# A decoder block on one core: the last half tile of gates handed over between blocks, and a merge with deeper, earlier loads

## The reference, cut to what matters

```python
h = rms_norm(x, g_mix) * (1.0 + sc1) + sh1
(a_q, a_k, a_v, conv_in, c_q, c_k, c_v, c_r, c_low,
 d_q, d_k, d_v, gate_logits) = split(h @ w_in)
y_a = dilated_attention_mixer(a_q, a_k, a_v, q_gain, k_gain) @ w_br_a
y_b = conformer_conv_mixer(conv_in, ...) @ w_br_b
y_c = gla_mixer(c_q, c_k, c_v, c_r, c_low, ...) @ w_br_c
y_d = stick_breaking_mixer(d_q, d_k, d_v) @ w_br_d
gates = sigmoid(gate_logits).reshape(bsz, seq, 4, 1024)
merged = gates[:,:,0]*y_a + gates[:,:,1]*y_b + gates[:,:,2]*y_c + gates[:,:,3]*y_d
x = x + gt1 * (merged @ w_out)
h = rms_norm(x, g_mlp) * (1.0 + sc2) + sh2
x = x + gt2 * (square(relu(h @ w_up)) @ w_down)
```

## Time and profile before

| what | us |
|---|---|
| median of the three runs | 2075.84 (2072.96 to 2077.95) |
| the profiled execution, its own time | 2075.17 |
| its span (first to last instruction) | 2073.4 |
| TensorE busy | 1989.8 (96% of the span) |
| front block, until TensorE starts in the stick block | 0 to 511.42 |
| stick block | to 711.35 |
| GLA block | to 914.53 |
| window block | to 1145.29 |
| close block: dense, y and merge | to 1309.1 |
| close block: output projection and MLP | to 2073.4 |

### The profile page before, as it was taken

The page is one execution under the profiler, slowest core; times in us unless marked ns, Lnnn a source line. Parts: engine busy times, 40 slices in busy tenths (PEclk is TensorE's granted clock), DMA queues, the critical chain, the costliest instruction groups (busy, mean ns, idle before and its releaser), DMA issues. The chain is left out here.

```text
span 2073.4 us, 24243 instructions
## 1 busy us (share of the span) xinstructions
PE 1989.8 (96%) x9416; PEld 1589.7 (77%) x9416; DVE 1239.4 (60%) x1631; ACT 695.8 (34%) x1087; POOL 249.6 (12%) x148
## 2 busy tenths in 40 slices
PE   5999999999999999989999788999999999999999
PEld 4787888877766677865788677788788888888887
DVE  6547575110465477343456377577877777777776
ACT  5311111132576432255553333333222212222221
POOL 0112122112221153125000000000000000000000
PEclk9999999999999999999999999999999999999999
DMA  8354554324211331252132655500211211111112
GB/s 277 86 172 128 169 155 119 92 82 149 86 45 51 130 106 47 87 217 103 45 116 67 205 187 177 177 11 10 92 46 46 67 46 51 52 61 41 51 41 92
DMA packets 197339, 206.47 MB, mean 100 GB/s; under 512 B 9402, under 2 KB 154938, under 8 KB 197226
## 3 DMA queue, kind: packets, MB, share of 16 engines
q1 hardware_dynamic: 197056, 204.85, 31.2%
q10 hardware_dynamic: 170, 0.07, 0.0%
HBM read 157.57 MB, written 47.32 MB: 99 GB/s over the span
## 5 line engine op out<-in xcount | busy, mean ns | idle before, releaser
L661 PE MATMUL dn_ps<-h_hi,dn_hi 128*128 128x512 f32 (+1 forms) x1120 | 460.4, 411 | 24.2 <-PEq L60 11.5
L663 PE MATMUL dn_ps<-h_hi,dn_lo 128*128 128x512 f32 (+1 forms) x1120 | 440.9, 394 | 0.0
L662 PE MATMUL dn_ps<-h_lo,dn_hi 128*128 128x512 f32 (+1 forms) x1120 | 440.8, 394 | 0.0
L661 PEld LDWEIGHTS dn_ps<-h_hi,dn_hi 128*128 128x128 f32 (+1 forms) x1120 | 211.4, 189 | 95.3 <-issue 44.9
L663 PEld LDWEIGHTS dn_ps<-h_hi,dn_lo 128*128 128x128 f32 (+1 forms) x1120 | 211.1, 188 | 48.3
L662 PEld LDWEIGHTS dn_ps<-h_lo,dn_hi 128*128 128x128 f32 (+1 forms) x1120 | 211.6, 189 | 45.8 <-issue 4.3
L139 POOL TENSOR_TENSOR dn_lo<-dn_raw,dn_hi 128x1024 fp32r<-128x1024 f32 (+1 forms) x69 | 169.3, 2455 | 620.8 <-ACT dn_hi L135 610.2
L156 ACT ACTIVATE dn_out<-dn_ps 128x512 f32<-128x512 f32 (+1 forms) x138 | 81.7, 592 | 450.3 <-PE dn_ps L663 442.6
L1505 DVE TENSOR_TENSOR tl_x<-tl_x,mg_ps_y 128x512 f32<-128x512 f32 x256 | 175.8, 687 | 89.4 <-PE mg_ps_y L663 82.6
L661 PE MATMUL mg_ps_y<-tl_slot_hi,tl_u_hi 128*128 128x512 f32 x480 | 187.0, 390 | 1.2 <-issue 1.2
L663 PE MATMUL mg_ps_y<-tl_slot_hi,tl_u_lo 128*128 128x512 f32 x480 | 186.8, 389 | 0.0
(11 more groups left out here) (375 smaller groups left out, 3406.1 us busy)
## 6 DMA issues: line engine op xcount, KB each, us to landing
dn_raw<-w_in_dram SPq DMA_DIRECT2D x70, 512.0 KB, 4.4
ada<-w_ada_dram SPq DMA_DIRECT2D x24, 1024.0 KB, 7.8
proj<-dn_out SPq DMA_DIRECT2D x72, 256.0 KB, 2.3
logits<-dn_out SPq DMA_DIRECT2D x64, 256.0 KB, 2.2
mg_gate<-logits SPq DMA_DIRECT2D x32, 512.0 KB, 4.9
tl_unit<-w_up_dram SPq DMA_DIRECT2D x64, 256.0 KB, 2.9
tl_unit<-w_down_dram SPq DMA_DIRECT2D x64, 256.0 KB, 2.7
wa_qk<-proj SPq DMA_DIRECT2D x6, 1024.0 KB, 15.9
```

Source lines behind the costliest of these rows:

```text
L661: nc.tensor.matmul(out, w_hi[:, t, :], x_hi[:, t, :], start=begin, stop=False, skip_group_check=reopened)
L662: nc.tensor.matmul(out, w_hi[:, t, :], x_lo[:, t, :], start=False, stop=False, skip_group_check=reopened)
L663: mm = nc.tensor.matmul(out, w_lo[:, t, :], x_hi[:, t, :], start=False, stop=end, skip_group_check=reopened)
```

## The change: what it does

At the end of each of the first four blocks the last half tile of dense work is computed, but its copy, the split that hangs on it and its store are moved to the head of the next block. GLA takes 23 half tiles instead of 22 and close 3 instead of 4; stick and window keep 20 and 18, so window's are now numbers 43 to 60. In GLA `lower` still runs up to the block's full count, so it includes the low part that half tile 42 calls for. In the merge, the logits get a ring of five buffers (three of `gate` and two more), half tiles are stored between the y loads, logits 0 and branch weights 1 are loaded among the y, logits 1 to 3 follow the last three y, later logits are issued four ahead, and `low_branch(n+1)` moves behind `merge(4n+1)`. Several buffers have new addresses so that branch weights 1 no longer lie on h. One wait of a later slot split (on `gain_done`) goes. The mathematics is the same.

```diff
@@ stage_front, SyncE and ScalarE
-                    for h in range(NH):
-                        dense.store(sp, j - 2, h)
+                    dense.store(sp, j - 2, 0)
+                    if j - 2 < N_TILES - 1:
+                        dense.store(sp, j - 2, 1)
...
-                for h in range(NH):
-                    dense.copy(act, j, h)
-                dense.split(act, j + 2)
+                dense.copy(act, j, 0)
+                if j < N_TILES - 1:
+                    dense.copy(act, j, 1)
+                    dense.split(act, j + 2)
@@ stage_stick, stage_gla, stage_window, stage_close
-    FROM = dense.served
+    FROM = dense.piece // 3
@@ stage_stick
-            dense.move(sp, FROM + HALVES)
+            dense.store(sp, dense.first_gate - 1, 1)
+            dense.move(sp, FROM + HALVES - 1)
...
+            dense.copy(act, dense.first_gate - 1, 1)
+            dense.split(act, dense.first_gate + 1)
...
-                dense.serve(act, FROM + halves_before(n))
-            dense.serve(act, FROM + HALVES)
+                dense.serve(act, FROM + min(HALVES - 1, halves_before(n)))
+            dense.serve(act, FROM + HALVES - 1)
@@ stage_gla
-    PREPARE, LEVEL, STATE, NORM = 8, 8, 2, 4
+    PREPARE, LEVEL, STATE, NORM = 8, 8, 2, 5
...
-            dense.move(sp, FROM + PREPARE + LEVEL + STATE + NORM)
+            dense.move(sp, FROM + PREPARE + LEVEL + STATE + NORM - 1)
...
-            dense.serve(act, FROM + PREPARE + LEVEL + STATE + NORM)
+            dense.serve(act, FROM + PREPARE + LEVEL + STATE + NORM - 1)
@@ stage_window
-            dense.move(sp, FROM + PREPARE + DURING + MERGING)
+            dense.move(sp, FROM + PREPARE + DURING + MERGING - 1)
...
-            dense.serve(act, FROM + PREPARE + DURING + MERGING)
+            dense.serve(act, FROM + PREPARE + DURING + MERGING - 1)
@@ stage_close
-    GATE_RING = 3
+    GATE_RING, LOGIT_RING = 3, 5
...
             def load_branch(n):
-                if n == 1:
-                    sp.wait_ge(dense.done, NH * len(dense.tiles))
...
             def load_logits(m):
-                if m < GATE_RING:
-                    sp.wait_ge(y_lo_ready, Y_TILES)
-                else:
-                    sp.wait_ge(used, m - GATE_RING + 1)
-                sp.dma_start(gate[:, m % GATE_RING], k.logits[m * P:(m + 1) * P, :]).then_inc(g_in[m % GATE_RING], 16)
+                if 1 <= m <= GATE_RING:
+                    sp.wait_ge(y_lo_ready, Y_TILES - GATE_RING + m)
+                elif m == LOGIT_RING - 1:
+                    sp.wait_ge(dense.done, NH * len(dense.tiles))
+                elif m >= LOGIT_RING:
+                    sp.wait_ge(used, m - LOGIT_RING + 1)
+                for h in range(NH):
+                    sp.wait_ge(dense.stored[h], 16 * (dense.first_gate + m - dense.early + 1))
+                sp.dma_start(logits_at(m), k.logits[m * P:(m + 1) * P, :]).then_inc(g_in[m % LOGIT_RING], 16)
...
             for t in range(Y_TILES):
                 load_y(t)
+                if t == 2:
+                    dense.move(sp, FROM)
+                    load_logits(0)
+                if t in (3, 6):
+                    dense.move(sp, FROM + min(HALVES, t // 3))
+                if t == 4:
+                    load_branch(1)
+            for m in range(1, GATE_RING + 1):
+                load_logits(m)
             dense.move(sp, FROM + HALVES)
-            load_branch(1)
-            for h in range(NH):
-                sp.wait_ge(dense.stored[h], 16 * (len(dense.tiles) - dense.early))
+            load_logits(LOGIT_RING - 1)
             for m in range(M):
-                load_logits(m)
+                if m >= 1 and m + LOGIT_RING - 1 < M:
+                    load_logits(m + LOGIT_RING - 1)
...
-                if m % 4 == 2 and m // 4 + 1 < N_TILES:
+                if m % 4 == 1 and m // 4 + 1 < N_TILES:
                     low_branch(m // 4 + 1)
```

More of the change, by code:

```diff
@@ L690, in stage_close @@
         merged = at("mg_merged", 0, [P, KT, S])
-        b_raw = [at("mg_br_raw0", 172, [P, Y_TILES, P]), at("mg_br_raw1", 32, [P, Y_TILES, P])]
-        b_hi = [at("mg_br_hi0", 177, [P, Y_TILES, P], F32R), at("mg_br_hi1", 37, [P, Y_TILES, P], F32R)]
-        b_lo = [at("mg_br_lo0", 182, [P, Y_TILES, P], F32R), at("mg_br_lo1", 42, [P, Y_TILES, P], F32R)]
+        b_raw = [at("mg_br_raw0", 172, [P, Y_TILES, P]), at("mg_br_raw1", 204, [P, Y_TILES, P])]
+        b_hi = [at("mg_br_hi0", 177, [P, Y_TILES, P], F32R), at("mg_br_hi1", 209, [P, Y_TILES, P], F32R)]
+        b_lo = [at("mg_br_lo0", 182, [P, Y_TILES, P], F32R), at("mg_br_lo1", 214, [P, Y_TILES, P], F32R)]
         y_hi = at("mg_y_hi", 92, [P, Y_TILES, S], F32R)
@@ L696, in stage_close @@
         gate = at("mg_gate", 187, [P, GATE_RING, S])
-        diag = [at("tl_diag1", 48, [P, KT, P]), at("tl_diag2", 204, [P, KT, P])]
+        gate_more = [at("mg_gate_first", 199, [P, S]), at("mg_gate_last", 44, [P, S])]
+        diag = [at("tl_diag1", 48, [P, KT, P]), at("tl_diag2", 32, [P, KT, P])]
         mj_hi = at("tl_mj_hi", 48, [P, 2, KT, P], F32R)
@@ L701, in stage_close @@
         raw = at("tl_raw", 64, [P, 2, KT * P])
-        raw_rest = [at("tl_raw_row4", 172, [P, D]), at("tl_raw_row5", 176, [P, D]), at("tl_raw_row6", 180, [P, D]), at("tl_raw_row7", 199, [P, D])]
+        raw_rest = [at("tl_raw_row4", 172, [P, D]), at("tl_raw_row5", 176, [P, D]), at("tl_raw_row6", 180, [P, D]), at("tl_raw_row7", 36, [P, D])]
         row_hi = [at("tl_wo_hi", 72, [P, 2, D], F32R), at("tl_wo_hi_rest", 92, [P, KT - 2, D], F32R)]
@@ L710, in stage_close @@
         xn_second = at("tl_xn_second", 36, [P, D])
-        SLOT_KB = (40, 44, 204, 212, 16, 20)
+        SLOT_KB = (44, 204, 208, 212, 16, 20)
         slot_hi = [at(f"tl_slot_hi{i}", kb, [P, 4, P], F32R) for i, kb in enumerate(SLOT_KB)]
@@ L722, in stage_close @@
         u_lo = [at("tl_u_lo", 56, [P, BF, S], F32R), at("tl_u_lo_last", 80, [P, BF, S], F32R)]
-        gain2 = at("tl_gain2", 208, [P, D])
+        gain2 = at("tl_gain2", 40, [P, D])
         ps_y = ctx.enter_context(nc.psum_tensor("mg_ps_y", [P, Y_RING, NH, HALF], F32))
@@ L727, in stage_close @@
         b_in = sems(nc, ctx, "mg_b_in0", "mg_b_in1")
-        g_in = sems(nc, ctx, *(f"mg_in{t}" for t in range(GATE_RING)))
+        g_in = sems(nc, ctx, *(f"mg_in{t}" for t in range(LOGIT_RING)))
         (y_hi_ready, y_lo_ready, b_hi_ready, b_lo_ready, y_done, gate_ready, gated, used) = sems(
@@ L754, in stage_close, with logits_at @@
         QUADS = [(0, 0), (1, 0), (0, 1), (1, 1)]
+        def logits_at(m):
+            s = m % LOGIT_RING
+            return gate[:, s % GATE_RING] if 1 <= s <= GATE_RING else gate_more[s // (LOGIT_RING - 1)][:, :]
         def pair(p):
@@ L976, in squash @@
             def squash(m):
-                act.wait_ge(g_in[m % GATE_RING], 16 * (m // GATE_RING + 1))
-                nc.scalar.activation(gate[:, m % GATE_RING], gate[:, m % GATE_RING], ACT.Sigmoid).then_inc(gate_ready, 1)
+                act.wait_ge(g_in[m % LOGIT_RING], 16 * (m // LOGIT_RING + 1))
+                nc.scalar.activation(logits_at(m), logits_at(m), ACT.Sigmoid).then_inc(gate_ready, 1)
             def split(t):
@@ L1304, in merge @@
                 y = ps_y[:, m % Y_RING, :, :].rearrange("p h c -> p (h c)")
-                g = gate[:, m % GATE_RING]
+                g = logits_at(m)
                 if i == 0:
```

2 lines of the change are left out of this document (removed).

## The result

The changed kernel takes 2052.39 us (median of 4 runs, 2052.14 to 2055.23). The kernel before, on the same chip, takes 2074.40 us. The ratio is 0.9895, with a 95% interval from 0.9878 to 0.9913: 18 to 25 us faster. The forecast was 2053, with a range from 2045 to 2062. The profiled execution took 2055.23 us itself (span 2053.5), 2.8 us above the median; before, the profiled one was 2075.17. In the new code `split_product` has lines 663 to 665 where it had 661 to 663.

A forecast was written before the change was run, and what follows sets the result against it. TensorE, busy 96% of the span, was taken as the bound. Terms -3.2, 0, +6.5, -1.6, -13.0 and -11.0 summed to -22.3 us against 2075.17, giving 2052.9, predicted as 2053, range 2045 to 2062.

The forecast's parts named there:

- Term 1: Front to stick: copy and split leave the path (-1.5 us) and the clock stays full (-1.7); -3.2 us.
- Term 2: Stick to GLA: the block ends with SyncE's store of the mixer output, so no change, 0 us.
- Term 3: GLA to window and window's start: GpSimd's low part delays the opening and the squares before `sums(1)`; +6.5 us.
- The wait of "10 us": Start of window: TensorE stands up to 10 us before `sums(1)`, with GpSimd's low part behind a late split.
- Term 4: Window to close: last copy and split lie 5.44 us before TensorE's end, idle falls from 3.03 to about 1.4; -1.6 us.
- Term 5: Opening of close, to the first product of group 1: product 4 at +39.5 instead of +52.5; -13.0 us.
- 5.44 of it is the half tile: Opening of close: 5.44 us of the -13.0 come from the half tile that GLA took over.
- The new wait of 3.7 us: Opening of close: the second half tile, 62, is reached at +5.4 but needs copy 60 at +9.1; 3.7 us idle.
- Term 6: The other seven groups of the merge: low-branch waits covered and their clock loss gone; -11.0 us.
- No stall in window: Rival: raw weights land early or GpSimd isn't what `sums(1)` waits for, term 3 about 0; 2046 us, chance 0.12.
- The merge gains less: Rival: loads compete with the y or the third group stays at VectorE's pace, 8 us lost; 2061 us, chance 0.22.
- VectorE as the bound: Rival: VectorE decides the seven merge groups, slower than before; 2086 us at 19 us a group, chance 0.03.

The follow-up runs named there:

- the repetition: The changed kernel run once more without any edit; 2050.25 us, ratio 0.9885.
- the late logits: Changed kernel, but logits from the sixth on wait until VectorE has used the gates three before, SyncE's order kept; 2065.86 us, ratio 0.9964.
- the half tile in close: Changed kernel with GLA put back to 22 half tiles and close to 4; 2046.54 us, ratio 0.9857.
- the squares first: Changed kernel, but in window GpSimd makes the first low part only behind the squares of tile 3; 2043.65 us, ratio 0.9843.
- the merge alone: The kernel before with the changed kernel's close block, GLA keeping 22 half tiles and close 4; 2046.86 us, ratio 0.9861.
- logits three ahead: Changed kernel with logits from the sixth on issued at their own step, once VectorE has used the gates three before; 2054.76 us, ratio 0.9898.
- both repairs: Changed kernel with GpSimd's squares of four tiles before the late low part, and tile 31's load ahead of window's two output stores; 2045.20 us, ratio 0.9865.

## Why the prediction was right, and where it was not

**The whole**: 2053 forecast, 2052.39 measured, and the sign and the range held. The parts did less well than the sum: that the two figures lie within 1 us of each other is luck, as parts that were off both ways cancelled.

**Term 1, front to stick, right.** -3.2 forecast, -3.26 in the traces (708.09 against 711.35). Idle was 1.19, and the clock came back to 1.00. This was not luck of one execution: behind 2.75 us of idle the first 6 us of the stick block ran at 0.72 in all three executions with the old crossing, behind 1.18 or 1.19 us at 1.00 in all eleven with the new one. The Trainium skill, "TensorE: Matmul & The Clock Gate", Part 1, which speaks of a number of slow matmuls that changes from run to run, would have left the 1.7 us out; at this crossing the traces do not agree. At the crossing into the window block they do, with 0.50 to 1.00 behind the same code (last section).

**Term 2, stick to GLA, right:** 1.74 us as before.

**Term 3, GLA to window and the start of window: mechanism right, size too small.** `sums(2)` was forecast to end at 957.5 - 3.2 = 954.3 and ended at 960.42. The chain was the one described, and the crossing itself had 2.84 and, repeated, 2.71 us of idle (forecast 2.7). The 6.1 us are, roughly: TensorE started window at 915.62 instead of 913.8 (1.8; the clock was 0.57 from 716 to 724, and in the repetition, where it was 0.79 at the same place of the block, GLA took 205.70 instead of 207.53, just the forecast's length); `sums(1)` took 3.78 us and not 1.88, as the clock was at 0.51 from 942 to 952 and I had booked a fifth of such a loss (1.9); `sums(2)` then waited 2.06 us for VectorE, a step that I took as free, and itself took 2.43 (0.5, nearly the 0.4 that was booked). The wait of "10 us" was 7.93 in this execution and 9.3 in the next. Of the 6.1 us 3.0 came back before the block's end, at one wait for VectorE (`wa_ps_third`, 3.0 us before and 1.0 now) and in the row behind it (2.12 us where it took 3.65). So GLA and window together cost +9.7, against the +6.5 of this term, and 1.8 of that is the clock in GLA.

**Term 4, window to close, wrong.** "The last copy and split lie 5.44 us before TensorE's end, with all that hangs on them": they did not. -1.6 forecast, 0 measured, idle 2.99. With the block's parity shifted by one half tile the load of the last gate tile had moved behind the store of the first half of the window output. I had followed copy and split, but not the load that the split waits for. The run with that load early had 1.58 us idle. That 2.99 isn't fixed either: in the kernel with the late logits the copy came 1.8 us earlier, counted back from TensorE's end, and idle was 1.59. Where GpSimd's low part falls does not explain it: there it met another addition of VectorE (2.77 us where 0.69 is usual) and held it up about as long as the small operation above. What brought the copy forward was not found out.

**Term 5, the opening of close: size right, its parts wrong.** -13.0 forecast with product 4 at +39.5; it came at +39.2, y 9 was split at +30.35 (forecast +30.4). But the step "5.44 of it is the half tile" failed. I wrote two lines earlier that y is later than TensorE; then a half tile less on TensorE can give nothing, and the half tile in close again showed it: same length with four as with three. The gain came from the order of the loads and from the earlier low branch. The new wait of 3.7 us before the second half tile was 0.49, because the branch weights landed sooner than in the kernel before (split at +4.3, not +7.3); in the repetition it was 1.18.

**Term 6, the seven groups, right.** 100.3 us forecast, 1291.60 - 1190.96 = 100.6 measured. Putting the low branch back cost 10 to 12 us, moving it alone gave 14.6. The third group keeps a wait of 0.66 us for a gate, the 0.6 that was left there.

**The sum.** GLA and window took 4.8 us more than forecast (terms 3 and 4). In close up to the last product of the merge the trace has 139.8 us against 163.8, the forecast -24.0. The rest of the kernel was 2.4 us shorter in this profile; 1.6 of that lie in the last part, which takes 738.3 or 739.9 us from one execution to the next in equal code. So 2055.23 against 2052.9 in the profiled execution, and the median of 2052.39 is nearer because the profiled one was the slowest of four.

**The rivals.** No stall in window: excluded by the 7.93 us; it exists with the squares first. The merge gains less: excluded, and the deeper ring of the logits, which that rival feared, costs nothing in the groups: it gives some 2.5 us there. VectorE as the bound: it was busy 79.98 of 100.64 us and never last for long, though the late logits show how near it is in the third group, where it works through row loads in program order.

## What to carry to other kernels

When work is shifted by one unit between stages, follow every engine's chain to its first cause, the loads too: an odd start moved a load behind a store in one place and a low part in front of squares in another. Work moved off a block is only worth its duration where TensorE, and not a transfer, ends that block's opening; ask what the destination waits for before booking the gain. And run the parts alone: here one part of the change was worth -29 us and the other +6, which the whole didn't show.

## What the runs showed of the hardware

The granted clock after an idle time of some 3 us depends on more than its length. At the front crossing 2.75 us lowered it every time. At the crossing into close, idle times of 2.74 to 3.06 us were followed by 1.00 in all eight executions that had them, but 3.34 us by 0.66. TensorE was busy at 1.00 through the 6 us before each of these idle times. The two rows are the merge alone at its front crossing, and the kernel with logits three ahead at its start of close:

```profile
510.65:516.65 6.00, 6.00 (x19) 4.81 (x20) 0.00 (x0) 1.60 (x3) 2.65 (x3) 0.72 0.83 297
```

```profile
1149.74:1154.74 5.00, 5.00 (x15) 3.96 (x16) 0.03 (x1) 0.62 (x1) 0.00 (x0) 0.66 0.70 201
```

At the crossing into the window block the same code and nearly the same idle time gave different clocks. Nine executions have the same program up to there, and 2.68 to 2.96 us of idle; their first 6 us of window ran at 0.50 (three), 0.72 (three), 0.76 and 1.00 (two), in no order of the idle times. The slowest and the fastest, the changed kernel behind 2.84 us and both repairs behind 2.68:

```profile
915.62:921.62 6.00, 6.00 (x14) 4.74 (x15) 3.64 (x14) 0.48 (x1) 0.48 (x2) 0.50 0.81 302
```

```profile
915.37:921.37 6.00, 6.00 (x26) 4.96 (x27) 3.64 (x14) 0.70 (x2) 0.45 (x2) 1.00 0.86 307
```

The clock also fell with no idle in front. In GLA TensorE was busy for all of 716 to 724 at 0.57; what stood before the fall was a row of eight matmuls with only 16 of 128 rows of weights, 4.12 us from 713.84.

Three VectorE operations of 128 by 8 elements took 2.56 us where they met GpSimd's low part of 2.40 us (the longest alone 2.41, the usual one 0.16), and 0.32 us five microseconds earlier, where they did not: one of them stood for as long as GpSimd worked. The Trainium skill, "SBUF — State Buffer", says that such an operation with two inputs and a GpSimd one exclude each other for a full instruction; the trace agrees.

SyncE's issue of one store took 9.29 us at 925.87, right behind the loads of the window block, while the core's transfers moved 421 GB/s; elsewhere it mostly takes 0.32 us. A load behind it, `load_v(2)`, left SyncE only at 935.21. Whether the queue was full or the engine waited for something else that the profile does not show was not tried.
